# A second mixer with a new order of work: attention and recurrent chains placed between weight units

## The reference

```python
def hybrid_mixer(h, w_in, conv_w, ...):
    proj = h @ w_in                                    # 1024 -> 7184
    (sb_q, sb_k, sb_v, conv_in, gla_q, gla_k, gla_v, gla_r, gla_lr, gate_logits) = split(proj)
    sb_out = stick_breaking_attention(sb_q, sb_k, sb_v)    # 8 heads of 64
    conv_out = conformer_conv(conv_in, ...)                # 512 channels, 31 taps
    log_alpha = log_sigmoid(gla_lr @ gla_w_alpha + gla_b_alpha) / 16
    gla_o = gla_chunked(gla_q, gla_k, gla_v, log_alpha)    # 4 chunks of 64 rows, state S_n from S_{n-1}
    gla_out = rms_norm(gla_o) * silu(gla_r)
    branch_d = einsum('bsgw,gwd->bsgd', stack([sb_out, conv_out, gla_out]), w_branch)
    return sum(sigmoid(gate_logits) * branch_d) @ w_out

def stick_breaking_attention(q, k, v):                 # per block of 128 queries
    z = q k^T * scale
    log_keep = where(earlier, log_sigmoid(-z), 0)
    log_stick = cumsum(log_keep, reverse=True) - log_keep
    w = where(earlier, exp(log_sigmoid(z) + log_stick), 0)
    return w v

def conformer_conv(u_glu, conv_w, conv_b, ln_g, ln_b):
    a, g = split(u_glu); u = a * sigmoid(g)
    y = depthwise causal convolution of u with 31 taps + conv_b
    return silu(layer_norm(y) * ln_g + ln_b)
```

## Time and profile before

| | us |
|---|---|
| median of 3 runs (2601.97 to 2607.53) | 2603.57 |
| profiled execution | 2602.84 |
| its span | 2601.1 |
| TensorE busy (matmul) | 2345.4 |
| VectorE busy | 1778.6 |
| ScalarE busy | 1405.5 |
| POOL busy | 219.2 |
| TensorE's mean granted clock (share of 2.4 GHz) | 0.949 |

### The profile page before, as it was taken

The page is one execution under the profiler, slowest core; times in us unless marked ns, Lnnn a source line. Parts: engine busy times, 40 slices in busy tenths (PEclk is TensorE's granted clock), DMA queues, the critical chain, the costliest instruction groups (busy, mean ns, idle before and its releaser), DMA issues.

```text
span 2601.1 us, 38772 instructions
## 1 busy us (share of the span) xinstructions
PE 2345.4 (90%) x10740; PEld 1907.0 (73%) x10740; DVE 1778.6 (68%) x2370; ACT 1405.5 (54%) x1821; POOL 219.2 (8%) x290
## 2 busy tenths in 40 slices
PE   6988799996988799996999987899999999779998
PEld 5776688875776587875887766778878878557887
DVE  3766688884776688886556786765565558777655
ACT  4543477772553477773445556354454455654544
POOL 0000000000000000000000590000000009500000
PEclk9998799998998799998999988999999999879999
DMA  6434499993533399994665643356656655334653
GB/s 204 151 118 124 136 348 341 340 334 126 170 102 122 106 349 340 356 340 143 208 190 154 186 135 114 123 186 185 186 184 185 183 180 156 98 114 146 196 184 105
DMA packets 277328, 497.31 MB, mean 191 GB/s; under 512 B 20448, under 2 KB 112656, under 8 KB 277184
## 3 DMA queue, kind: packets, MB, share of 16 engines
q1 hardware_dynamic: 273280, 482.92, 56.4%
q0 software_dynamic: 3904, 12.70, 1.6%
HBM read 494.50 MB, written 1.05 MB: 191 GB/s over the span
## 4 chain that ended last, share of the span: by engine, by line
PE 76%; DVE 10%; DVEq 5%; ACT 4%; issue 3%; DMA 1%; ACTq 1%; SPq 0%; POOLq 0%
PE g_bank L497 15%; PE g_bank L498 15%; PE g_bank L499 15%; PE s_bank L499 8%; PE s_bank L497 8%; PE s_bank L498 8%; DVE w_lo L486 2%; PE t_bank L1409 1%; DVE conv_y L2210 1%; DVEq L2204 1%; DMA w_raw<-in_w_in_dram 1%; DVE xt_lo L553 1%; PE t_bank L1550 1%; DVEq L1883 1%; PE t_bank L538 1%
## 5 line engine op out<-in xcount | busy, mean ns | idle before, releaser
L486 DVE TENSOR_TENSOR w_lo<-w_raw,w_hi 128x1024 fp32r<-128x1024 f32 x929 | 1116.2, 1229 | 449.6 <-ACT w_hi L481 422.8
L481 ACT ACTIVATE w_hi<-w_raw 128x1024 fp32r<-128x1024 f32 x929 | 969.2, 1059 | 557.0 <-PE g_bank L499 296.3
L497 PE MATMUL g_bank<-w_hi,xt_hi 128*128 128x512 f32 (+1 forms) x1152 | 471.1, 409 | 34.5 <-DVEq L561 13.7
L498 PE MATMUL g_bank<-w_lo,xt_hi 128*128 128x512 f32 (+1 forms) x1152 | 460.4, 400 | 0.0
L499 PE MATMUL g_bank<-w_hi,xt_lo 128*128 128x512 f32 (+1 forms) x1152 | 459.2, 399 | 0.0
L497 PEld LDWEIGHTS g_bank<-w_hi,xt_hi 128*128 128x128 f32 x1152 | 227.3, 197 | 89.6 <-issue 35.9
L499 PEld LDWEIGHTS g_bank<-w_hi,xt_lo 128*128 128x128 f32 x1152 | 225.7, 196 | 48.5
L498 PEld LDWEIGHTS g_bank<-w_lo,xt_hi 128*128 128x128 f32 x1152 | 227.2, 197 | 44.9
L497 PE MATMUL s_bank<-w_hi,xt_hi 128*128 128x512 f32 x640 | 252.7, 395 | 0.0
L499 PE MATMUL s_bank<-w_hi,xt_lo 128*128 128x512 f32 x640 | 249.8, 390 | 0.0
L498 PE MATMUL s_bank<-w_lo,xt_hi 128*128 128x512 f32 x640 | 249.4, 390 | 0.0
(11 more groups left out here) (333 smaller groups left out, 2723.6 us busy)
## 6 DMA issues: line engine op xcount, KB each, us to landing
w_raw<-in_w_in_dram SPq DMA_DIRECT2D x192, 512.0 KB, 4.5
w_raw<-in_moe_w_gate_dram SPq DMA_DIRECT2D x128, 512.0 KB, 5.3
w_raw<-in_moe_w_up_dram SPq DMA_DIRECT2D x128, 512.0 KB, 5.1
w_raw<-in_moe_w_down_dram SPq DMA_DIRECT2D x128, 512.0 KB, 5.2
w_raw<-in_ffn_w_gate_dram SPq DMA_DIRECT2D x176, 256.0 KB, 2.9
w_raw<-in_ffn_w_up_dram SPq DMA_DIRECT2D x176, 256.0 KB, 3.1
w_raw<-in_ffn_w_down_dram SPq DMA_DIRECT2D x88, 512.0 KB, 3.8
w_raw<-in_w_branch_dram SPq DMA_DIRECT2D x40, 512.0 KB, 3.9
```

The costliest lines, as they stand in the source:

```text
L481: nc.scalar.activation(half_of(w_hi, u, h), half_of(w_raw, u, h), ACT.Copy).then_inc(hi_ready, 1)
L486: nc.vector.tensor_tensor(half_of(w_lo, u, h), half_of(w_raw, u, h), half_of(w_hi, u, h).bitcast(F32), ALU.subtract).then_inc(lo_ready, 1)
L497: nc.tensor.matmul(dst, a_hi, b_hi, start=first, stop=False)
L498: nc.tensor.matmul(dst, a_hi, b_lo, start=False, stop=False)
```

## The change

One table of units (`UNITS2`) now says in which order the 29 projection, decay and gate units come, and `plan_mixer2` writes every step of the stage by itself: `unit` (TensorE), `hi` (ScalarE's split) and `lo` (VectorE's split) are steps of their own and need not stand together; so are `taps`, the outputs `proj_out`, `lr_out`, `gate_out`, and the transposes `taps_t`, `conv_t`, `qk`.

- The attention starts behind the fifth projection block (`S_V` is now block 4) and not behind the narrow unit, and each group has two units around it. One tap stands behind each group's scores. `stick` comes ahead of the second unit's splits, `probs_t` behind both units.
- Taps: three behind each of four units, one in each group, the other 15 behind the attention, up to unit 25; `conv_back` follows there. It was ahead of the recurrent chain.
- The recurrent chain (`alpha` to `gla_out`) stands between gate units ahead of `conv_back`. The decay input goes to `t_bank`; `gla_o` is kept in `logit` and `lin_qt` in `gains`, so that they don't overwrite the convolution's tiles.
- `conv_norm`: subtraction and gain in one instruction per tile, scale and bias in another (three before).
- Branch order 0, 2, 1; the attention's transposes stand between the last gate units, those of the recurrent branch and the convolution behind them.
- ScalarE preloads the set that holds exponential and logarithm behind `qk` and at `alpha`, and the one with silu at the first `gate_out`.
- `convolve` itself, its three channel blocks on VectorE and POOL's one, are as before.

```diff
-PROJ2_ORDER = (3, 4, 0, 1, 5, 2, 6, 7)
+PROJ2_ORDER = (3, 4, 0, 1, 2, 5, 6, 7)
+BRANCH2_ORDER, BRANCH2_CHUNK = (0, 2, 1), (8, 0, 4)
+UNITS2 = ([("proj", i, half) for i in range(5) for half in range(2)] + [("lr", 0, 0)] +
+          [("proj", i, half) for i in (5, 6) for half in range(2)] + [("gate", 0, half) for half in range(2)] +
+          [("proj", 7, half) for half in range(2)] + [("gate", n, half) for n in range(1, 6) for half in range(2)])
 def plan_mixer2():
...
-        step("scores", n_s=1, **here)
-        if i:
-            step("probs_t", n_t=1 + before["tt"], **before)
-        step("soft", **here)
-        step("scan", **here)
-        gate()
-        if i:
-            step("values", n_t=1, **before)
-        step("stick", **here)
-        gate((20 + 3 * i, min(23 + 3 * i, TAPS)))
...
+    plain(3)
+    step("qk", n_t=4)
+    plain(3)
+    out("proj", 4)
...
+    for i, what in enumerate((("proj", 5), ("proj", 6), None), 1):
+        group("scores", i)
+        group("soft", i)
+        take(1)
+        unit()
+        hi()
+        group("scan", i)
+        group("stick", i)
+        group("values", i - 1)
+        if i == 1:
+            out("lr", 0)
+        if what:
+            out(*what)
+        lo()
+        unit()
+        hi()
+        lo()
+        group("probs_t", i)
...
+    step("alpha", n_t=2)
+    unit()
+    step("alpha_end")
+    hi()
+    lo()
+    take(1)
+    step("gla_q", n_t=1)
+    plain()
+    out("gate", 1)
+    step("decay", n_t=2)
+    step("k_dec")
+    plain(2)
+    step("states", n_t=2, half=0)
+    plain(2)
+    out("gate", 2)
+    step("states", n_t=2, half=1)
+    plain(2)
+    hi()
+    step("gla_out", n_t=2)
+    unit()
+    lo()
+    take(3)
+    out("gate", 3)
+    plain(3)
     step("conv_back", n_t=2)
-    step("alpha_end")
-    gate()
+    plain()
     step("conv_norm")
...
+    out("gate", 4)
+    plain()
+    step("branches_t", n_t=2)
+    plain()
+    out("gate", 5)
...
-        lin_qt = conv_in[:, :, :].rearrange(flat)[:, 0:512].rearrange("p (h n) -> p h n", h=2)
+        lin_qt = gains[:, 0, 0:512].rearrange("p (h n) -> p h n", h=2)
-        gla_o = conv_y[:, :, :].rearrange("p (t a) n -> p t (a n)", t=TT)
+        gla_o = logit[:, :, :].rearrange("p (t a) n -> p t (a n)", t=TT)
...
+                        act.preload_act_table_set("natural_log_exp_and_others")
...
                     elif kind == "conv_norm":
-                        dve.wait_ge(rstd_ready, At(4 + 4, (l, 11)).value(1, 1))
...
-                            dve.tensor_scalar(out_[tt], t_bank[tf.slot(2)][:, :], mean_var[:, tt, 0:1], rstd[:, tt:tt + 1],
-                                              ALU.subtract, ALU.mult).then_inc(t_free[tf.slot(2)], 1)
+                        dve.wait_ge(rstd_ready, At(4 + 5, (l, 11)).value(1, 1))
                         dve.drain()
                         for tt in range(TT):
-                            dve.tensor_tensor(out_[tt], out_[tt], conv_row[:, 0:512], ALU.mult)
...
+                            dve.scalar_tensor_tensor(out=part, in0=part, scalar=rstd[:, tt:tt + 1], in1=conv_row[:, 512:1024],
+                                                     op0=ALU.mult, op1=ALU.add)
```

More of the change, by code:

```diff
@@ L175 @@
 PLAN1_VECTOR = vector_order(PLAN1)
+UNITS2 = ([("proj", i, half) for i in range(5) for half in range(2)] + [("lr", 0, 0)] +
+          [("proj", i, half) for i in (5, 6) for half in range(2)] + [("gate", 0, half) for half in range(2)] +
+          [("proj", 7, half) for half in range(2)] + [("gate", n, half) for n in range(1, 6) for half in range(2)])
 def plan_mixer2():
-    t, g, s, steps = 4 + 1 + 2 + 4, 16 + 2, 0, []
-    halves = iter([(n, half) for n in range(6) for half in range(2)])
+    t, g, s, steps, fills, done = 4, 2, 0, [], {("proj", 0): 0}, 0
+    units = iter(enumerate(UNITS2[2:], 2))
+    n_hi = n_lo = 2
     groups = [(0, 0), (0, 1), (1, 0), (1, 1)]
@@ L187, in step, with unit @@
         t, g, s = t + n_t, g + n_g, s + n_s
-    def gate(taps=(0, 0)):
-        n, half = next(halves)
+    def unit():
+        k, (what, i, half) = next(units)
         if half == 0:
-            step("gate", n_g=2, n=n, half=0, taps=taps)
-        else:
-            first = [st["g"] for st in steps if st["kind"] == "gate" and st["n"] == n][0]
-            steps.append(dict(kind="gate", t=t, g=first, s=s, n=n, half=1, taps=taps))
-    for i, (grp, tt) in enumerate(groups):
-        here = dict(grp=grp, tt=tt, n=i)
-        before = dict(grp=groups[i - 1][0], tt=groups[i - 1][1], n=i - 1)
-        step("scores", n_s=1, **here)
-        if i:
-            step("probs_t", n_t=1 + before["tt"], **before)
-        step("soft", **here)
-        step("scan", **here)
-        gate()
-        if i:
-            step("values", n_t=1, **before)
-        step("stick", **here)
-        gate((20 + 3 * i, min(23 + 3 * i, TAPS)))
@@ L211, in plan_mixer2, with hi, lo, take @@
-    step("probs_t", n_t=1 + tt, **here)
-    step("alpha", n_g=2)
-    step("values", n_t=1, **here)
+            fills[what, i] = g
+        step("unit", n_g=2 * (half == 0), k=k, what=what, i=i, half=half, fill=fills[what, i])
+    def hi():
+        nonlocal n_hi
+        step("hi", k=n_hi)
+        n_hi += 1
+    def lo():
+        nonlocal n_lo
+        step("lo", k=n_lo)
+        n_lo += 1
+    def take(n):
+        nonlocal done
+        step("taps", taps=(done, done + n))
+        done += n
@@ new lines, in out, with group, plain @@
+    def out(what, i):
+        step(what + "_out", i=i, fill=fills[what, i])
+    def group(kind, i):
+        step(kind, n_t={"probs_t": 1 + groups[i][1], "values": 1}.get(kind, 0), n_s=(kind == "scores"),
+             grp=groups[i][0], tt=groups[i][1], n=i)
+    def plain(taps=0):
+        unit()
+        hi()
+        lo()
+        if taps:
+            take(taps)
+    plain()
+    plain()
+    out("proj", 1)
+    step("conv_u")
+    plain()
+    step("taps_t", n_t=1)
+    plain()
+    step("conv_t", n_t=2)
@@ new lines, in plan_mixer2 @@
+    out("proj", 2)
+    plain(3)
+    plain(3)
+    out("proj", 3)
+    plain(3)
+    step("qk", n_t=4)
+    plain(3)
+    out("proj", 4)
+    group("scores", 0)
+    group("soft", 0)
+    take(1)
+    unit()
+    hi()
+    group("scan", 0)
+    group("stick", 0)
+    lo()
+    unit()
+    hi()
+    lo()
+    group("probs_t", 0)
+    for i, what in enumerate((("proj", 5), ("proj", 6), None), 1):
[12 more added lines that the diff above has]
+        lo()
+        unit()
+        hi()
+        lo()
+        group("probs_t", i)
@@ new lines, in plan_mixer2 @@
+    out("gate", 0)
+    unit()
+    hi()
+    lo()
+    take(2)
+    group("values", 3)
+    out("proj", 7)
+    step("alpha", n_t=2)
+    unit()
+    step("alpha_end")
+    hi()
+    lo()
+    take(1)
+    step("gla_q", n_t=1)
+    plain()
+    out("gate", 1)
[7 more added lines that the diff above has]
+    plain(2)
+    hi()
+    step("gla_out", n_t=2)
+    unit()
+    lo()
+    take(3)
@@ L214, in plan_mixer2 @@
+    out("gate", 3)
+    plain(3)
     step("conv_back", n_t=2)
-    step("alpha_end")
-    gate()
+    plain()
     step("conv_norm")
-    step("gla_q", n_t=1)
-    step("decay", n_t=2)
-    gate()
-    step("states", n_t=4)
-    gate()
-    step("gla_out", n_t=2)
-    gate()
-    step("branches_t", n_t=4)
-    assert t == 36 and g == 32 and s == S_MIX2
+    out("gate", 4)
+    plain()
+    step("branches_t", n_t=2)
+    plain()
+    out("gate", 5)
+    assert next(units, None) is None and done == TAPS and t == 36 and g == 30 and s == S_MIX2
@@ L561, in dve_xt @@
                 nc.vector.drain().then_inc(xt_ready, 1)
[L564 to L565 removed]
+        EARLY_BRANCH = [(tt, 2) for tt in range(TT)]
+        LATE_BRANCHES = [(tt, j) for j in range(2) for tt in range(TT)]
         MERGED = [[(tt, blk) for tt in range(TT)] for blk in range(2)]
```

294 lines of the change are left out of this document (149 added, 145 removed).

## The result

The changed kernel takes 2582.35 us in the median of 4 runs (2580.70 to 2585.88); the kernel before took 2602.77 beside it on the same chip (2601.95 to 2607.53). The ratio is 0.992, 95% interval 0.9902 to 0.9937: 20.4 us faster, 10.2 a layer, where 23.4 a layer were forecast. The time lies inside the range of the prediction (2521 to 2593) and within 4 us of rival B's price (2579). But the two layers were to gain 46.8 us and gained 20.4: the way was right, the size was not.

The account below looks back on a forecast made before the run. VectorE's work and waits, not matmul throughput, bound the stage: last tap at 1604.6 plus tail 24.5 gives 1629.1 instead of 1652.5, 23.4 us per layer; 2602.84 - 2 x 23.4 = 2556.0 us (2535 to 2572; with most of A 2521 to 2593).

Parts of the forecast that it names:

- rival B: Attention and convolution stage: only removed table loads (10.3 us) and 1.4 count, 11.7 us per layer, 2579 us; chance 0.19.
- Other waits of VectorE: VectorE's waits up to the last tap besides softplus: decay, lo half, hand-overs, hi halves; 10.6 us, bounds 5 to 23.
- the decay product's: Decay product moved from a g bank to a t bank: 0 us, bounds -2 to +2, one bank wait.
- VectorE's busy time to the last tap: VectorE's queue from the convolution's input to its last tap: 135.3 of 151.6 us of work, 16.3 behind.
- Softplus waits: VectorE's four waits for ScalarE's softplus, one per attention group: 6.0 us in sum instead of 18.4.
- The tail: From VectorE's last tap to the first branch product: transposes, units 26 to 28 and late transposes, 24.5 us.
- The stretch behind: The stretch behind the first branch product, at TensorE's pace: unchanged at 60.2 us.
- The wait at the convolution's transposes: Expected sign: one long TensorE wait there, 12 to 20 us, ended by VectorE's last tap.
- POOL: Interference from POOL computing its channel block beside the attention: 1.3 us more for VectorE, between 0 and 4.
- Rival A: Same stage: TensorE, not VectorE, is the bound; 43.5 us per layer gained, 2516 us; chance 0.16.
- Rival C: The convolution becomes the end and the kernel slower: last tap after 1628.0, 2609 to 2630 us; chance 0.09.
- D: TensorE's attention waits only reappear at the convolution; the stage keeps its 141.7 us, 2603 us; chance 0.04.

Follow-up runs that it names:

- all three moves: Changed kernel with lr_out behind group 0's probs_t, convolution's way back two units later, and values 3, proj 7 and alpha ahead of two taps: 2554.13 us.

## Why the forecast was wrong

*The step that failed is "Other waits of VectorE", 10.6 us with bounds 5 to 23.* It measured 35.2 - 4.8 = 30.4, above its upper bound: 14.5 for hi halves, 4.8 at the decay (2.2 and 2.6, where 2.2 and 1 were put), 3.1 for late scores, the rest short hand-overs. The bound had all of the old waits for hi halves but only 5 us for the rest. Being 19.8 us too small, less what was too high elsewhere, it put the last tap 17 us late (170.3 from the convolution's input instead of 153.2) and took 13.2 of the 23.4 us a layer by the medians. (In layer 0's trace the first branch product comes 226.8 us behind the mixer's start, with 234.3 before and 210.9 forecast. Of the 22.1 us between the two profiled executions 2.2 lie ahead of that mixer, in a part that the change leaves alone.) I had it near the lower end because the hi halves were now queued ahead of the stick exponential. That they are, but a hi half also waits for TensorE to release its half of the ring (22.5 us of ScalarE's time up to the last tap, 18.8 with all three moves), and TensorE had stopped on something else.

*What it stopped on.* Two banks released late, which the prediction put at nothing (the low-rank one) and at 0 with bounds of -2 to +2 (the decay product's): by the low-rank copy (6.4 us, and 2.6 for the start at the lower clock) and by the copy of values 3 (4.2). I had read the new order for the work that stands in VectorE's queue, not for who frees each bank that TensorE needs next. With these two and the convolution's transposes moved, the time is 2554.1: the moves give 14.1 us a layer, against 13.2 missing. In layer 0's trace the last tap is 12.3 earlier (202.2 to 189.9 behind the mixer's start) and the tail about 3 shorter, which the forecast hadn't counted on; so it is luck that this kernel comes within 2 us of the forecast. The moves explain 12.3 of the last tap's 17 us. The remaining 5 were not split by a run and stay open. A part of them is VectorE's first wait for a hi half, which none of the moves changes; ahead of it ScalarE has the convolution's input and a projection's output to write. Before and now:

```profile
1452.22 1.23 DVE L486 TENSOR_TENSOR w_lo<-w_raw,w_hi 128x1024 fp32r<-128x1024 f32 x1 [3.53 <-ACT w_hi L481]
```

```profile
1450.55 2.36 DVE L579 TENSOR_TENSOR w_lo<-w_raw,w_hi 128x1024 fp32r<-128x1024 f32 x2 [4.64 <-ACT w_hi L574]
```

Of this wait 0.8 us lay behind the convolution's input before (1451.4), and 2.6 lie there now (1447.9).

*What held.* VectorE's busy time to the last tap, 135.2 for 135.3 (a sum over some 200 instructions from rows of before). Softplus waits, 4.8 for 6.0. The tail, 24.6 for 24.5. The stretch behind, 60.1 for 60.2 by the windows; they don't end at the same instruction, though: up to the next feed-forward's transposes it is 56.4 us, 57.7 before, at a granted clock of 1.00 for 0.97. The wait at the convolution's transposes, 13.6 (12 to 20 expected). Nine table loads a mixer. TensorE's waits for the exponential were to fall below 6 us and are 7.4; VectorE was to be over 85% busy and is 79%, as it was.

*POOL.* The 1.3 us forecast stand for what the change adds: wide scans went from 747 to 815 ns and narrow ones from 424 to 504, 1.2 us over all sixteen, while taps got shorter. POOL's whole cost, old and new, is 6.7 us a layer. The Trainium skill ("SBUF — State Buffer", Who interferes with whom) has the two exclude each other for a whole instruction. The trace shows less: POOL adds 44 ns to the mean tap and 143 to the mean wide scan, and in both layers no single tap took over 0.77 us and no subtraction over 1.54, against 0.48 and 1.22 alone. That is at most 0.32 us more, about half a POOL product of 0.60.

*Rival A* (TensorE alone, 2516): without the last 12 taps and with all moves the kernel still takes 2539. *Rival B* came nearest with 2579, for a wrong reason: it counted 10.3 us a layer for eight loads, and nine cost 4.15; and it held the ring's coupling for a floor, while the same ring with the same work runs at 2554. Its sign, waits for hi halves above 18 us, did come: 19.5 over the extent of the earlier trace rows. *Rival C*: its mechanism is there (the last tap comes late, 1618.2 in the trace), but short of the point from which it decides, 1628. *D*, that TensorE's waits only appear again elsewhere, had the smallest chance but one part of it is true: TensorE stands 33.8 us where it stood 36.1. Its time, 2603, isn't, since the stage still got 6.2 us shorter.

## What to carry over

When work is put in a new order, list for each bank that the busiest engine takes next the instruction that frees it, and what stands before that one in its own queue; a copy of 0.4 us behind the wrong wait cost 5.3 us a layer. An idle engine's waits for its neighbour in a ring aren't its own: look for the first engine that stopped. Add up the busiest engine's waits over the same stretch before and after: here the largest item fell from 19.3 to 7.4 us, while all of TensorE's idle time only fell from 36.1 to 33.8. And an edit's worth depends on the order that it is made in: three taps in each group gained 5.3 us in one and lost 10.0 in another.

## What the runs showed of the chip

- In the changed kernel's two layers, stops of TensorE of 4.2 to 6.4 us at the low-rank bank and at the alpha product were followed by a start at half clock (matmuls 0.43 us apart instead of 0.227): the next unit's 24 took 8.4 and 8.5 us in the first layer, 8.6 and 7.1 in the second, instead of 5.73. Shorter stops at the alpha product went both ways: 1.5 us with lr_out moved, then 8.24; 1.0 with alpha moved, then 8.39; 1.2 with all three moves, then 5.75. So by these rows the length of the stop alone does not tell which level follows. With two stops fewer the granted clock from the convolution's input to the last tap was 0.97 instead of 0.88.
- A table load of 1283 ns cost 0.46 us of the kernel's time on average, nine of them in a stage where ScalarE is busy half of the time.
